# A two-block transformer on one core: wave tables a step sooner, scan products behind the softmax mask, gates copied first and put through the sigmoid in two groups

## The reference, cut to what matters

```python
h = rms_norm(x, norm1_g[l])
z = h @ w_in[l]
(cq, ckv, kpe, gq, gk, gv, glr, gr, su, gates) = split_in(z)
o_a = mla_mixer(cq, ckv, kpe, ...)      # softmax attention, 8 heads
o_b = gla_mixer(gq, gk, gv, glr, gr, ...)   # gated linear attention, 4 heads
o_c = s5_mixer(su, ...)                 # complex diagonal recurrence, 32 groups x 64 states
g = jax.nn.sigmoid(gates + gate_b[l]).reshape(B, L, N_BRANCH, D)
merged = (g[:, :, 0] * (o_a @ w_br_mla[l])
          + g[:, :, 1] * (o_b @ w_br_gla[l])
          + g[:, :, 2] * (o_c @ w_br_s5[l]))
x = x + merged @ w_out[l]
x = x + jnp.square(jax.nn.relu(rms_norm(x, norm2_g[l]) @ w_ff1[l])) @ w_ff2[l]
```

## Time and profile before

| | |
|---|---|
| median of three runs | 2354.32 us (2353.38 to 2358.48) |
| the profiled execution | 2355.58 us, its span 2353.8 us, so 1.8 us lie outside the span |
| busy share of the span | PE 84%, DVE 48%, ACT 33%, POOL 1% |
| mean granted clock of PE | 0.917 of full |

### The profile page before, as it was taken

The page is one execution under the profiler, slowest core; times in us unless marked ns, Lnnn a source line. Parts: engine busy times, 40 slices in busy tenths (PEclk is TensorE's granted clock), DMA queues, the critical chain, the costliest instruction groups (busy, mean ns, idle before and its releaser), DMA issues.

```text
span 2353.8 us, 31309 instructions
## 1 busy us (share of the span) xinstructions
PE 1985.3 (84%) x12631; PEld 1468.9 (62%) x12631; DVE 1136.0 (48%) x2228; ACT 769.9 (33%) x1252; POOL 28.8 (1%) x49
## 2 busy tenths in 40 slices
PE   6999999867666566666666899889999998999999
PEld 4987789634323232332332576669988866689887
DVE  3888876411111111110111376767875567876854
ACT  4448863200000000000000134644554425644542
POOL 0000000000000000000000200000000200000000
PEclk8999999988788887887787999999999999999999
DMA  9545756999999999999999833324555434225552
GB/s 339 188 165 181 221 172 226 401 428 426 427 426 427 427 426 427 426 427 427 427 427 427 305 120 108 125 70 145 182 185 206 121 118 161 72 82 187 197 179 90
DMA packets 147058, 619.23 MB, mean 263 GB/s; under 512 B 6800, under 2 KB 25776, under 8 KB 122208
## 3 DMA queue, kind: packets, MB, share of 16 engines
q1 hardware_dynamic: 145504, 615.89, 66.9%
q0 software_dynamic: 1408, 1.29, 0.3%
HBM read 622.40 MB, written 1.05 MB: 265 GB/s over the span
## 4 chain that ended last, share of the span: by engine, by line
PE 65%; DMA 19%; DVE 9%; ACT 5%; issue 1%; SPq 1%; DVEq 0%; ACTq 0%
PE pb L184 19%; DMA ring<-in_w 11%; PE pb L424 9%; DMA ar<-in_w 6%; PE pb L1365 6%; PE pb L1340 5%; PE pb L425 4%; PE pb L1304 2%; PE pb L637 1%; PE pb L639 1%; PE pb L638 1%; PE pb L520 1%; PE pb L519 1%; PE pb L518 1%; DMA ring<-in_w_ada 1%
## 5 line engine op out<-in xcount | busy, mean ns | idle before, releaser
L184 PE MATMUL pb<-ar,ring 128*128 128x256 f32 (+1 forms) x1696 | 396.5, 391 | 16.4 <-ACT ar L2399 9.9
L184 PEld LDWEIGHTS pb<-ar,ring 128*128 128x128 f32 (+1 forms) x1696 | 322.7, 194 | 76.7 <-issue 15.7
L424 PE MATMUL pb<-act,parts 128*128 128x512 f32 x944 | 336.4, 398 | 0.1
L1340 PE MATMUL pb<-ring,ar 128*32 128x512 f32 x1264 | 256.0, 650 | 70.5 <-DMA ring<-in_w 46.0
L425 PE MATMUL pb<-act,parts 128*128 128x256 f32 x944 | 264.9, 281 | 0.0
L1340 PE MATMUL pb<-ar 128*32 128x512 f32 x784 | 202.4, 668 | 45.2 <-DMA ar<-in_w 26.7
L2317 DVE TENSOR_TENSOR parts<-ring,parts 128x2048 fp32r<-128x2048 f32 x72 | 161.6, 2287 | 105.5 <-ACT parts L2310 105.5
L1365 PE MATMUL pb<-ring,ar 128*32 128x512 f32 x608 | 143.0, 722 | 76.8 <-DMA ring<-in_w 53.6
L424 PEld LDWEIGHTS pb<-act,parts 128*128 128x128 f32 x944 | 177.4, 188 | 39.8 <-DVE parts L2317 0.4
L1587 DVE TENSOR_TENSOR ar<-ar,pb 128x512 f32<-128x512 f32 x16 | 11.0, 688 | 382.2 <-PE pb L1340 382.2
L1422 ACT ACTIVATE ar<-pb 128x512 f32<-128x512 f32 x16 | 9.6, 597 | 533.7 <-PE pb L1365 533.7
(11 more groups left out here) (492 smaller groups left out, 3738.8 us busy)
## 6 DMA issues: line engine op xcount, KB each, us to landing
ring<-in_w SPq DMA_DIRECT2D x109, 2048.0 KB, 29.4
ar<-in_w SPq DMA_DIRECT2D x72, 2048.0 KB, 30.9
ring<-in_w_in SPq DMA_DIRECT2D x36, 2048.0 KB, 8.6
ring<-in_w_ff SPq DMA_DIRECT2D x32, 2048.0 KB, 8.2
ring<-in_w_ada SPq DMA_DIRECT2D x12, 2048.0 KB, 13.8
ring<-in_w SPq DMA_DIRECT2D x10, 1024.0 KB, 12.1
ring<-in_w_ssm_out SPq DMA_DIRECT2D x4, 2048.0 KB, 8.2
ring<-in_w_out SPq DMA_DIRECT2D x4, 2048.0 KB, 8.5
```

The source lines that it names most:

```text
L184: ins = e.matmul(out, l, r, start=(i == 0), stop=(i == len(pairs) - 1))
L424: e.matmul(p, wh, both, start=first, stop=False)
L1340: ins = e.matmul(k.pb[b][32 * j:32 * j + 32, :], v.xg[:, kt, 32 * j:32 * j + 32], w[j][:, kt, :], start=(kt == 0), stop=(kt == 7))
```

## The change

Four edits, the same in both layers.

1. *Waves one step sooner.* In the four items whose scan stage is followed by a mask (`MASKED` = 2, 3, 4, 5), DVE does `fraction(u + 1)` ahead of the scans of item u, and ACT does `table(u + 1)` in the scan stage and no longer in the out stage.
2. *Scan products behind the mask.* In these four items the scan products (now `remodulate`) come behind the mask.
3. *Gates emptied by copies.* ACT empties gate0 to gate15 with Identity and bias. Two instructions of 8 x 256 elements, `gate_group`, apply the sigmoid in place: to gate0 to gate7 in step 22, to gate8 to gate15 in step 29. DVE's gate products of branches 0 and 1 wait for them (`sigmoids`). Gates 16 to 23 keep the sigmoid.
4. *One unit ahead of the roots.* In step 7 ACT empties one of the step's three units ahead of `head_roots`.

```diff
@@ weave
         if leading:
             units.more(tiles)
+        if settled and PHASES[2 * step] == ("head_roots", 1):
+            units.more(1)
+            units.settle()
+            tiles -= 1
         main(*PHASES[2 * step])
...
+MASKED = [u for u in range(8) if PHASES[2 * SPACE.index(("scan", u)) + 1][0] == "mask"]
@@ layer_ac
-                    o.done(e.activation(v.gate[:, m % 16, :], acc, ACT.Sigmoid, bias=k.par(f"gateb{l}")[:, m:m + 1]), k.s("unit_ac"))
+                    o.done(e.activation(v.gate[:, m % 16, :], acc, ACT.Sigmoid if m >= 16 else ACT.Identity, bias=k.par(f"gateb{l}")[:, m:m + 1]), k.s("unit_ac"))
...
+        elif phase == "inside":
+            gate_group(0)
...
+    def gate_group(br):
+        units.upto(f"gate{8 * br + 7}")
+        x = v.gate[:, 8 * br:8 * br + 8, :]
+        o.done(o.after().activation(x, x, ACT.Sigmoid), k.s("sigmoids"))
...
-        elif step == "scan" and u in (2, 4, 6):
-            gelu(u // 2 - 1)
-        elif step == "out" and u < 7:
+        elif step == "scan":
+            if u in MASKED:
+                table(u + 1)
+            if u in (2, 4, 6):
+                gelu(u // 2 - 1)
+        elif step == "out" and u < 7 and u not in MASKED:
             table(u + 1)
         elif step == "last" and u == 1:
             gelu(3)
         elif step == "last" and u == 2:
-            units.upto("gate15")
+            gate_group(1)
@@ layer_ve
+        if u in MASKED:
+            open_scan.append((u, done))
+        else:
+            remodulate(u, done)
+
+    def remodulate(u, done):
+        s, c = v.sn[u % 2], v.cs[u % 2]
         t1 = o.done(o.after(done[0]).tensor_tensor(v.pr, v.sx, c, ALU.mult))
...
         elif step == "scan":
+            if u in MASKED:
+                fraction(u + 1)
             scan(u)
-            if u < 7:
+            if u < 7 and u not in MASKED:
                 fraction(u + 1)
...
-        after_unit(k, e, l, f"gate{8 * br + m}")
+        if br < 2:
+            e.wait_ge(*k.at("sigmoids", 2 * l + br + 1))
+        else:
+            after_unit(k, e, l, f"gate{8 * br + m}")
...
+    def main_then_scan(phase, i):
+        main(phase, i)
+        if open_scan:
+            remodulate(*open_scan.pop())
+
-    weave(units, main, space, first_branch)
+    weave(units, main_then_scan, space, first_branch)
```

More of the change, by code:

```diff
@@ L55 @@
     "front_high": ("counted", 4), "front_low": ("blocks", 3), "unit_high": ("n2_turned", 4), "unit_low": ("w_rt", 16),
+    "sigmoids": ("h_moe", 8),
     "gss": ("hg", 9), "st": ("logits_turned", 1), "mm_state": ("place", 2),
@@ L2769, in fraction @@
         o.done(o.after().tensor_tensor(s, s, c, ALU.subtract), k.s("fraction"))
+    open_scan = []
     def demodulate(u):
```

## The result

| | before | after |
|---|---|---|
| median | 2354.14 us (six runs, 2351.94 to 2358.48) | 2325.49 us (six runs, 2324.66 to 2331.48) |
| profiled execution, its span | 2355.58, 2353.8 us | 2325.95, 2324.1 us |
| mean granted clock of PE | 0.917 | 0.924 |

The ratio is 0.9882, with a 95% interval of 0.9868 to 0.9897; the medians differ by 28.65 us. The page of the changed kernel answers to the earlier trace rows: PE is busy for 14.8 us less although it makes the same products, ACT for 28.2 us less.

What follows compares the result with a forecast made beforehand. PE, busy 84% of the span, was taken as the bound, so gains were its idle gaps and half-clock time: 10.0 + 19.1 - 1.5 - 3.6 - 0.5 = 23.5 us, giving 2331 us, range 2323 to 2342.

Steps and rivals of the forecast that it cites:

- the forecast case: Whole kernel: all terms come as summed, 2331 us, with its own range of 2326 to 2338; chance 0.65.
- item 3: PE's gap ahead of item 3's outputs grows to 4.3 us; with the small wait 0.75 lost per layer, 1.5 in all.
- ties: Items 4 and 5: PE and DVE start from the same score product and tie within tenths; 0.5 us lost in all.
- the unit ahead of the roots: PE's 2.77 us gap ahead of gate0 goes with its half clock: 5.75 us in layer 0, 4.22 in layer 1.
- the wait ahead of gate9: PE's gap, 3.26 us in layer 0 and 2.07 in layer 1, closes because gate7 is emptied 4.5 us sooner.
- the wait ahead of the transposes of block 3: PE's 0.92 us wait for probabilities closes in each layer, as two loads, 2.57 us, leave ACT's path.
- The long sigmoids: Two per layer on ACT, 1.9 us each plus a 1.28 load, hidden; the first ready some 9 us early.
- a fall at item 3: PE's clock drops to half rate behind item 3's gap in each layer, 2.5 us each; 3.6 lost net.
- Slower: Items 2 to 5: the products' deferral is paid whole with a clock fall at each, 2373 us; chance 0.04.
- the tie is lost: Items 4 and 5, both layers: mask takes 1 us longer, PE waits and clock falls, 14 us, 2345; chance 0.12.
- ACT's part does nothing: PE's later gaps reopen where DVE is next; only the unit's 10.0 us is gained, 2344 us; chance 0.07.
- The rival without a clock fall: Item 3's new gap doesn't cost the clock: 28.5 us gained, 2326 us; chance 0.12.

Runs made afterwards that it cites:

- edit 4 alone: Kernel before the change, with only one unit emptied by ACT ahead of the roots: 2345.15 us, ratio 0.9964 to before.
- edit 3 alone: Kernel before the change, with only gate0 to gate15 emptied by copies and two long sigmoids: 2343.07 us, ratio 0.9957 to before.
- edits 1 and 2 alone: Kernel before the change, with only fraction and table a step sooner and scan products behind the mask: 2344.24 us, ratio 0.9963 to before.
- edits 3 and 4: Kernel before the change, with gate copies, long sigmoids and the unit ahead of the roots, orders unchanged: 2333.08 us, ratio 0.9914 to before.
- the trace with the copies on ACT: Changed kernel with item 3's scan products ahead of the mask, and ACT instead of DVE copying turned probabilities of blocks 1 to 3: 2319.31 us, ratio 0.9854 to before.
- that without edit 2: Changed kernel with the scan products ahead of the mask again, all else kept: 2326.10 us, ratio 0.9873 to before.

## Why the prediction was right, and where it was off

The time gained was 28.65 us where 23.5 were forecast: inside the stated range, and half a us beyond the range that the forecast case had for itself, 2326 to 2338.

**Idle time: the gaps as forecast, the sum in part by luck.** In the prediction's terms the removed gaps are 9.25 us in layer 0 and 8.06 in layer 1, less 1.5 for item 3 and 0.5 for ties: 15.3. Measured 15.4. All of these gaps went. But item 3 took 2.04 and the ties nothing; small waits of 0.15 to 0.41 us that I had left out went too, 1.15 in all; one of 0.60 came in layer 1; and the changed kernel has 0.4 more of idle time that no row's bracket shows. These errors cancel. The mechanism of each part was found alone: the unit ahead of the roots by edit 4 alone; the wait ahead of gate9 by edit 3 alone (half of it) and by edits 1 and 2 alone (all of it); the wait ahead of the transposes of block 3 by edit 3. ACT empties gr1 in the time in which it waited anyway:

```profile
1438.95 0.38 ACT L2410 ACTIVATE ar<-pb 128x256 f32<-128x256 f32 x1 [9.76 <-PE pb L1987]
1439.35 1.28 ACT L2434 ACT_TABLE_LOAD   x1
1442.20 0.49 ACT L2434 ACTIVATE ar<-ar,misc 128x8 f32<-128x8 f32 x2 [1.57 <-DVE ar L2679]
```

**The long sigmoids: as forecast.** The 1.9 us taken from the copy in the earlier trace rows and the load of 1.28 are what they took. No engine waits for them: in layer 0 DVE's first gate product starts 8.5 us behind the end of the first one, where some 9 were forecast. The rows of this first one:

```profile
1531.89 1.28 ACT L2478 ACT_TABLE_LOAD   x1
1533.18 1.91 ACT L2478 ACTIVATE ar<-ar 128x2048 f32<-128x2048 f32 x1
```

The sigmoid starts 0.01 us behind its load. The Trainium skill ("ScalarE: Activation LUTs", section "What ACT_TABLE_LOAD costs") adds about 1.38 us of drain to every load of 1283 ns, 2.66 in all; these rows show the 1.28 us and no drain behind them. The instruction ahead of the load ends at 1531.87, 0.02 us before it, so none is seen there either.

**Item 3: the gap to 0.03 us, its neighbour not.** Forecast 4.3 and measured 4.33, and 4.34 in layer 1. The small wait was to go from 0.80 to 0.35 and went to 0.60, so 1.02 us per layer are lost, not 0.75. The aside that without the deferral PE would wait only 1.1 us was wrong: it waited 2.43. I had counted fraction and mask, 3.15 us, as the deferral, but edit 1 takes the fraction away from there in any case. What is left is the copy and the mask, 1.9. Where the fraction stands behind the products too (edits 3 and 4), the wait is 1.69.

**The clock: the term that was mis-sized.** I wrote 2.5 us for a fall at item 3 in each layer, so 3.6 lost net of the 1.36 that stood in layer 1. It fell in both, as forecast, and cost 1.64 each; and layer 1's fall before the change had cost 1.64 with gate8's share counted, so the net loss is 1.64 instead of 3.6. That is 2.0 us of what the forecast missed. By its terms the busy time was to fall by 8.2 us, 11.8 of falls less 3.6; it fell by 14.0.

**The rest of these 5.8 us.** Before the change the clock also fell at the outputs of item 7 in layer 1, which no term held:

```profile
2069.56 2.42 PE L2174 MATMUL pb<-ar 128*32 128x256 f32 x16 [2.02 <-DVE ar L2801]
...
2073.10 4.28 PE L184 MATMUL pb<-ar,ring 128*128 128x256 f32 x16
```

That is 0.50 + 0.56 = 1.1 us. 2.8 us remain. They may lie in the overlap of PE's rows: unbroken, gate0's row of 3.62 us is followed by the next after 3.54; before the change it was 6.64, so the fall cost 3.10 and not the 2.98 that the row lengths gave. Some 0.1 us ahead of each of a dozen gaps and 0.1 behind would make up most of the 2.8. This is an account worked out from rows, not an experiment.

**The rivals.** No time was lost to ties: the outputs of items 4 and 5 start when the unit ahead of them ends. "Slower" and "the tie is lost" fell with the 1.92 us rows without a gap at items 4 and 5. "ACT's part does nothing" fell with the run of edit 3. The rival without a clock fall named nearly the measured time, 2326, but its mechanism did not happen: the clock fell in both layers.

## What to carry to other kernels

When one engine sets most of the time, list its gaps, and ask of each what stands ahead of the releasing instruction in the releasing engine's queue and need not stand there: an emptying that waits behind a long wait for something else, a table load for a function that could be applied later to eight tiles at once. Those gaps can be summed before the change is made, and they went as summed. What the clock gives back with them, half of the gain here, was read far less well (8.2 us forecast, 14.0 measured). A gap between two steps of a chain on another engine (here DVE, item 3) is of another kind: filling it with other work gave back 1.7 of 4.3 us, while work taken off that chain, or moved into that chain's own idle time, paid nearly in full. Test parts alone and by leaving one out: of four edits here one, the deferral of the scan products, earned nothing on top of the others and cost 1.5 us a layer up to item 7, though it would have paid without edit 1.

## What the runs showed of the hardware

The length of a gap alone doesn't tell whether PE's clock falls. The 4.33 to 4.52 us gap of item 3 was followed by slow rows in all eight stretches that had it. But one of 3.11 was followed by a slow row in two cases of four, one of 2.02 at item 7 in some runs and not in others, and the 1.84 us ahead of gate9 by a row of 5.41 with edit 3 alone and by one of 3.72 with edits 3 and 4:

```profile
1493.12 3.72 PE L185 MATMUL pb<-ar,ring 128*128 128x256 f32 x16 [1.83 <-ACT ar L2407]
```

The rule of the Trainium skill on the clock ("TensorE: Matmul & The Clock Gate", section "HAM oscillation — how this bites in real kernels"), that a long enough idle gap brings the half rate and each one pays anew, holds for the 4.33 us gap; it doesn't tell these short ones apart, and no run here isolates what does. At the item 3 gap of layer 0 the clock is still full in the idle stretch from 1487 to 1488. It falls only when PE has started again, to the lower level, 0.50 (1.2 GHz), and is back near full (0.95) in the stretch from 1492 to 1493:

```profile
1487.00:1488.00 1.00, 0.00 (x0) 0.00 (x0) 0.99 (x2) 1.00 (x5) 0.00 (x0) 1.00 1.04 430
1488.00:1489.00 1.00, 0.96 (x8) 0.56 (x10) 0.87 (x2) 0.93 (x3) 0.00 (x0) 0.84 0.99 401
1489.00:1490.00 1.00, 1.00 (x6) 0.37 (x4) 0.00 (x0) 0.00 (x0) 0.00 (x0) 0.50 1.06 438
...
1492.00:1493.00 1.00, 1.00 (x6) 0.86 (x5) 1.00 (x3) 0.00 (x0) 0.00 (x0) 0.95 0.06 16
```

The parts that no edit touches differ from run to run by more than some edits are worth. From the start of the program to the unit with 16 columns of layer 0 the traces show 1416.64 to 1421.01 us. From gate16 of layer 0 to that unit of layer 1 it is 318.81 us in the trace with the copies on ACT and 323.29 in that without edit 2, where the clock is 0.91 between 1820 and 1860 us. So an edit worth 1 us is hardly seen in the times. In the stretch of a trace it can be, if the falls of the clock, up to 1 us each, are read out first.
